# Expert weights in transfers of one whole matrix each: 2 MB as 128 runs of 16 KB in place of 512 runs of 4 KB, in a ring of eight slabs

## What is computed

```python
def hier_moe(x, w_rg, b_rg, w_re, b_re, w1, w3, w2):
    ...
    def expert_block(args):
        xb, e = args
        hdn = jax.nn.silu(xb @ w1[e]) * (xb @ w3[e])
        return hdn @ w2[e]
```

## Time and profile before

| | before |
|---|---|
| median of 3 runs | 1940.58 us (1939.97 to 1940.86) |
| the profiled execution | 1940.22 us, of which its span is 1938.4 us |
| PE busy | 1519.8 us, 78% of the span |
| DVE, ACT busy | 615.2 us, 420.9 us |
| DMA | 525.01 MB, 271 GB/s over the span |
| TensorE clock granted, mean | 0.916 of full |

### The profile page before, as it was taken

One profiled execution on the slowest core, in us unless ns is written; L12 is line 12 of the kernel. 1 busy time (PEld: TensorE's weight loads), 2 busy tenths in 40 slices (PEclk: granted clock), 3 DMA queues, 4 the chain that ended last, 5 costly groups with the idle time before them and its releaser, 6 DMA issues.

```text
span 1938.4 us, 22240 instructions
## 1 busy us (share of the span) xinstructions
PE 1519.8 (78%) x9046; PEld 1056.9 (55%) x9046; DVE 615.2 (32%) x1084; ACT 420.9 (22%) x616; POOL 4.7 (0%) x5
## 2 busy tenths in 40 slices
PE   7998979666666666666666567665999999989996
PEld 7788768522333123321333223331788878769996
DVE  3687931510111001110111101110453568244653
ACT  3554020410010000100100001000421332234542
POOL 0000000000000000000000000000000000000000
PEclk9999989788898889988998889888999999989998
DMA  9432344199999999999999999999432314325530
GB/s 318 156 131 96 143 151 183 41 365 410 409 410 410 410 410 410 410 410 409 410 410 410 410 410 410 410 409 400 174 126 87 131 44 174 123 96 189 195 116 23
DMA packets 164418, 525.01 MB, mean 271 GB/s; under 512 B 6514, under 2 KB 14834, under 8 KB 164356
## 3 DMA queue, kind: packets, MB, share of 16 engines
q1 hardware_dynamic: 164048, 523.39, 69.8%
q10 hardware_dynamic: 308, 0.78, 0.1%
HBM read 523.10 MB, written 1.05 MB: 270 GB/s over the span
## 4 chain that ended last, share of the span: by engine, by line
PE 55%; DMA 20%; DVE 10%; SPq 9%; ACT 2%; issue 2%; DVEq 0%; ACTq 0%
DMA ring<-in_w 20%; PE psum L323 15%; SPq L1259 9%; PE psum L998 6%; PE psum L1013 5%; PE psum L381 5%; PE psum L382 5%; PE psum L383 5%; PE psum L1042 3%; DVE arena L746 3%; PE psum L1032 3%; PE psum L344 2%; PE psum L603 1%; DVE shared L1757 1%; PE psum L1394 1%
## 5 line engine op out<-in xcount | busy, mean ns | idle before, releaser
L1013 PE MATMUL psum<-ring,arena 128*32 128x512 f32 x1536 | 224.9, 722 | 133.3 <-DMA ring<-in_w 119.2
L381 PE MATMUL psum<-parts 128*128 128x256 f32 (+1 forms) x832 | 246.2, 296 | 11.4 <-DVE parts L459 6.8
L382 PE MATMUL psum<-parts 128*128 128x256 f32 (+1 forms) x832 | 243.2, 292 | 0.0
L383 PE MATMUL psum<-parts 128*128 128x256 f32 (+1 forms) x832 | 243.1, 292 | 0.0
L323 PE MATMUL psum<-arena,ring 128*128 128x256 f32 x960 | 214.9, 386 | 11.8 <-DMA ring<-in_w_in 11.3
L323 PEld LDWEIGHTS psum<-arena,ring 128*128 128x128 f32 x960 | 184.9, 194 | 38.5 <-issue 13.0
L1013 PEld LDWEIGHTS psum<-ring,arena 128*32 128x32 f32 x1536 | 49.9, 125 | 285.3 <-DMA ring<-in_w 174.1
L381 PEld LDWEIGHTS psum<-parts 128*128 128x128 f32 x832 | 161.6, 194 | 20.6 <-issue 13.7
L383 PEld LDWEIGHTS psum<-parts 128*128 128x128 f32 x832 | 162.0, 195 | 2.1
L382 PEld LDWEIGHTS psum<-parts 128*128 128x128 f32 x832 | 162.0, 195 | 1.9
L1213 DVE TENSOR_TENSOR shared<-shared,psum 128x512 f32<-128x512 f32 x16 | 11.0, 687 | 460.7 <-PE psum L1013 460.7
(11 more groups left out here) (207 smaller groups left out, 1451.3 us busy)
## 6 DMA issues: line engine op xcount, KB each, us to landing
ring<-in_w SPq DMA_DIRECT2D x128, 2048.0 KB, 23.6
shared<-in_w SPq DMA_DIRECT2D x64, 2048.0 KB, 23.4
ring<-in_w_in SPq DMA_DIRECT2D x18, 2048.0 KB, 8.8
ring<-in_w_ffn_gate_up SPq DMA_DIRECT2D x11, 2048.0 KB, 8.0
ring<-in_w_gate SPq DMA_DIRECT2D x8, 2048.0 KB, 8.9
ring<-in_w_ffn_down SPq DMA_DIRECT2D x5, 2048.0 KB, 7.8
ring<-in_w_out SPq DMA_DIRECT2D x4, 2048.0 KB, 8.1
ring<-in_w_gla_out SPq DMA_DIRECT2D x2, 2048.0 KB, 8.2
```

The costliest lines, as they stand in the source:

```text
L381: pe.matmul(out, w[0], x[0], start=start, stop=False)
L382: pe.matmul(out, w[0], x[1], start=False, stop=False)
L383: return pe.matmul(out, w[1], x[0], start=False, stop=stop)
L1013: m = pe.matmul(ps[slots, bank, :], V.picked[:, k, slots], part[:, e, j, :], start=(k == 0), stop=(k == DT - 1))
```

## The change

It makes one transfer out of one whole matrix of one expert (16 KB in one run for each partition), and a ring of eight slabs, counted over a pair of quads (24 slabs). The ring has two places more, slots 6 to 7 and 8 to 9 of `shared`; what lay there (the router's numbers, the memory's squares and root) moves to other slots. PE waits for each of a product's four slabs at the first contraction tile, and frees each at the last one. Eight loads are issued ahead of the loop, not six. The loop over quads becomes one over pairs of quads, with the body in a function.

```diff
@@ block1_pe @@
-    for i in (2, 3):
-        pe.drain().then_inc(S(f"moe_read{i}"), 1)
+    for i in (0, 1):
+        pe.drain().then_inc(S(f"moe_read{i}"), FREED)
...
         pe_slab_tiles(K, pe, B, R, f"co{s}", tiles("co", 4 * s, 4), cu)
-        pe.drain().then_inc(S(f"moe_read{s}"), 1)
+        pe.drain().then_inc(S(f"moe_read{2 + s}"), FREED)
+        if s == 0:
+            pe.drain().then_inc(S("moe_read4"), FREED)
...
-        pe.drain().then_inc(S(f"moe_read{4 + s}"), 1)
+        pe.drain().then_inc(S(f"moe_read{5 + s}"), FREED)
+    pe.drain().then_inc(S("moe_read7"), FREED)
...
-CUTS = 4
-SETS = [(name, cut) for name in ("w1", "w3", "w2") for cut in range(CUTS)]
-RSETS = RING
+SLABS3 = [(name, e) for name in ("w1", "w3", "w2") for e in range(QUAD)]
+RSLABS = 8
+PAIR = 2
+USES = PAIR * len(SLABS3) // RSLABS
+FREED = 2
+PLACES = (4, 5, 2, 3, 6, 0, 1, 7)
...
+    def wait_landed(self, eng, n, i):
+        eng.wait_ge(self.landed(i), n * (16 * USES) + 16 * (i // RSLABS + 1))
+    def wait_passed(self, eng, n, i):
+        eng.wait_ge(self.passed(i), n * USES + i // RSLABS + FREED + 1)
@@ moe_pe @@
-            for w, bank in enumerate(MOE_BANK["up"]):
-                for cut in range(CUTS):
-                    i = CUTS * w + cut
-                    pe.wait_ge(S(f"moe_landed{i % RSETS}"), n * 32 + 16 * (i // RSETS + 1))
-                    part = moe_set(K, i, DT // CUTS)
-                    for j in range(DT // CUTS):
-                        k = DT // CUTS * cut + j
-                        for e in range(QUAD):
-                            slots = slice(e * SLOTS, (e + 1) * SLOTS)
-                            m = pe.matmul(ps[slots, bank, :], V.picked[:, k, slots], part[:, e, j, :],
-                                          start=(k == 0), stop=(k == DT - 1))
-                    m.then_inc(S(f"moe_read{i % RSETS}"), 1)
+        for name, bank in zip(("w1", "w3"), MOE_BANK["up"]):
+            at = [ring.index(half, name, e) for e in range(QUAD)]
+            w = [ring.slab(i, DT) for i in at]
+            for k in range(DT):
+                for e in range(QUAD):
+                    if k == 0:
+                        ring.wait_landed(pe, pair, at[e])
+                    slots = slice(e * SLOTS, (e + 1) * SLOTS)
+                    m = pe.matmul(ps[slots, bank, :], V.picked[:, k, slots], w[e][:, k, :],
+                                  start=(k == 0), stop=(k == DT - 1))
+                    if k == DT - 1:
+                        m.then_inc(ring.passed(at[e]), 1)
...
@@ moe_sp @@
-    w = {name: d[name].rearrange("e (p h k) n -> h p e (k n)", p=P, h=CUTS) for name in ("w1", "w3", "w2")}
+    w = {name: d[name].rearrange("e (p k) n -> p e (k n)", p=P) for name in ("w1", "w3", "w2")}
...
-        sp.dma_start(moe_set(K, i, 1).rearrange("p e k n -> p e (k n)"), w[name][cut, :, bass.ds(first, QUAD), :])\
-          .then_inc(S(f"moe_landed{i % RSETS}"), 16)
+        sp.dma_start(ring.slab(i, 1), w[name][:, bass.ds(first + (i // len(SLABS3) * QUAD + e), 1), :])\
+          .then_inc(ring.landed(i), 16)
-    for i in (2, 3, 0, 1, 4, 5):
-        load(i, 0, 1)
+    for i in range(RSLABS):
+        load(i, 0, 0, FREED)
...
-    sp.wait_ge(S("moe_read1"), rounds * NQ * 2 + 1)
+    sp.wait_ge(ring.passed(3), rounds * pairs * USES + FREED)
```

More of the change, by code:

```diff
@@ L972, in moe_pe @@
     pe.wait_ge(S("mem_squares"), 1)
[L973 removed]
+    pe_group(K, pe, B, "mem_ms", [K.c("j1024")] * DT, [K.tiles(3, DT)[:, j, :] for j in range(DT)])
     pe.wait_ge(S("chosen"), 1)
@@ L1045, in moe_pe @@
+    with pe.Fori(0, rounds) as r:
+        with pe.Fori(0, NQ // PAIR) as q:
+            for half in range(PAIR):
+                quad(r * (NQ // PAIR) + q, half)
     pe.drain().then_inc(S("moe_over"), 1)
@@ new lines, in moe_dve, with quad @@
+    ring = MoeRing(K)
+    last_of = lambda half, name: ring.index(half, name, QUAD - 1)
+    def quad(pair, q, half):
+        n = pair * PAIR + half
+        first = q * (PAIR * QUAD) + half * QUAD
+        for t in range(TT):
+            dve.tensor_tensor(by_slot(V.sel[:, t, :]), wide(K.c("slot_iota"), QUAD),
+                              last(V.place[:, t, bass.ds(first, QUAD)], SLOTS), ALU.is_equal).then_inc(S("sel_built"), 1)
+        dve.wait_ge(S("sel_built"), n * 4 + 2)
+        for t in range(TT):
+            dve.tensor_tensor(by_slot(V.wsel[:, t, :]), by_slot(V.sel[:, t, :]),
+                              last(V.weight[:, t, bass.ds(first, QUAD)], SLOTS), ALU.mult).then_inc(S("sel_built"), 1)
+        dve.wait_ge(S("picked"), n * 2 + 1)
+        dve.tensor_copy(K.A(3, 512), ps[:, MOE_BANK["pick"][0], :]).then_inc(S("picked_dve"), 1)
+        dve.wait_ge(S("silu"), n + 1)
+        ring.wait_passed(dve, pair, last_of(half, "w3"))
+        dve.tensor_tensor(V.hidden, V.hidden, ps[:, MOE_BANK["up"][1], :], ALU.mult).then_inc(S("gated"), 1)
+        ring.wait_passed(dve, pair, last_of(half, "w2"))
+        dve.tensor_copy(K.A(4, 512, 1024), ps[:, MOE_BANK["down"][0], :]).then_inc(S("y_dve"), 1)
+        for j, bank in enumerate(MOE_BANK["put"]):
+            dve.wait_ge(S("put"), n * 4 + j + 1)
+            part = K.A(2, 512, 512 * j)
+            dve.tensor_tensor(part, part, ps[:, bank, :], ALU.add).then_inc(S("total_added"), 1)
+        dve.wait_ge(S("total_added"), n * 4 + 5)
@@ L1223, in moe_dve @@
+    with dve.Fori(0, rounds) as r:
+        with dve.Fori(0, NQ // PAIR) as q:
+            for half in range(PAIR):
+                quad(r * (NQ // PAIR) + q, q, half)
         ins = dve.tensor_scalar(K.A(5, TT * NE, 576), K.A(5, TT * NE, 576), -float(SLOTS), None, ALU.add)
```

234 lines of the change are left out of this document (118 added, 116 removed).

## The result

| | before | after |
|---|---|---|
| median, 4 runs each on one chip | 1940.28 us (1938.07 to 1940.86) | 1896.50 us (1891.92 to 1900.74) |
| the profiled execution | 1940.22 us, span 1938.4 | 1897.18 us, span 1895.4 |
| PE busy | 1519.8 us | 1558.4 us |

The ratio of after to before is 0.978, with a 95% interval of 0.9765 to 0.9795: faster, by 43.8 us where 32 were forecast. The time lies inside the range, in the middle of its lower half.

A forecast was written before the change was run, and what follows sets the result against it. DMA was taken to bound the expert stage. 396.6 + 0.3 + 3.7 + 184 x 4.94 (909.0) + 8.7 = 1318.3 against 1350.7, 32.4 us earlier, so 1940.2 became about 1908 us; range 1886 to 1930.

The forecast's parts named there:

- The bound and the mechanism: Expert stage: DMA sets the pace at 410 GB/s; 16 KB packets pay the 9.5 ns price per packet less often.
- The slab: Expert stage: one 2.097 MB transfer was to take 4.94 us (424.5 GB/s) for 5.12 before, with 184 left to move.
- consts2's 415 GB/s: Only row with packets above 4 KB: 81 packets of 7680 B over 1.5 us, meaning 5.05 us a slab.
- the two long rows: DMA rates in long runs, 387 GB/s for 2 KB packets and 410 for 4 KB; continued to 16 KB, 4.89 us a slab.
- The second argument: Mid-transfer rates of 400 and 425 GB/s give 4.70 us of data, plus 0.19 us per transfer: 4.89 us a slab.
- The start: Expert stage's beginning: first load in the loop 5.3 us later, at 396.6 plus 0.3, but eight slabs early, not six.
- the drains: First block on PE: two more drains, 0 to 0.7 us in all, taken as 0.3.
- Worth 2 x 5.12 = 10.2 us: Two more slabs loaded early, in DMA's idle stretch between 340 and 390 us, leave 184 to move, not 186.
- The end: After the last landing all of w2's product remains: 8.7 us, bounds 7.1 to 13.6, where one cut took 3.39.
- All behind it is unchanged: Everything after the last w2 product, the second block included, was to keep its time, so the 32.4 us carry through.
- The PE loop: Rival, chance 0.05: low clock stretches w2's landing to w1's release, loop 65.5 us, 2007 us total; expected loop 54.1 under 59.3.
- the latency: Term of the loop between PE and DMA in each quad: 2.7 us, 7.8 to landing for a lone slab less 5.1 of data.

The follow-up runs named there:

- e3: The changed kernel with two experts' matrices in one 4 MB transfer, still in 16 KB runs: median 1893.31 us, ratio 0.9769.
- e2: The changed kernel with the seventh and eighth loads held back until w1's first slab is freed: median 1907.97 us, ratio 0.9837.
- e9: The changed kernel with five unread matmuls before the second block's 2.35 us wait and 32 products widened from 8 to 64 columns: 1892.55 us.
- e4: The changed kernel with the last quad's w2 loaded in four cuts of 4 KB per expert: median 1894.06 us, ratio 0.9768.
- the two edits: In the second block, five unread matmuls before the 2.35 us wait, and 32 products widened from 8 to 64 columns; on the kernel of before, 1932.96 us.
- e11: The kernel of before with five unread matmuls before the second block's 2.35 us wait and 32 products widened to 64 columns: 1932.96 us, ratio 0.9968.

## Why the prediction was right, and where its sizes were off

**The bound and the mechanism were right.** The stage was bound by DMA, a run of 16 KB goes as one packet, and the price of a packet is paid once for it. The run with 4 KB packets shows that nothing else in the change makes up the gain.

**The slab was mis-sized**, and this is most of the error. The sum took 4.94 us, "a third of the way to the one short row that speaks against them", consts2's 415 GB/s over 1.5 us. Measured are (1302.3 - 397.0 - 3.7) / 184 = 4.90 us, or 428 GB/s. The line through the two long rows had said 4.89, and 429. So 7.4 us of the 10.6 us by which the forecast was above the profiled pair come from having let 81 packets outvote two long rows. The second argument, from 3 us at 425 GB/s, gave the same 4.89 by way of a cost per transfer that e3 shows not to be there; that it agreed was chance, and should not have counted as support.

**The start was right, in part by luck.** Forecast 396.9 for the first load in the loop, measured 397.0. But w1's product starts at 389.62 for 389.00, 0.6 us later where 0.3 was taken for the drains, and the load goes out 0.33 us after its end where 0.53 was taken; the two misses cancel. (PE's times ahead of the stage differ by 0.6 us the other way at 278 us, before any of the drains added, so the 0.6 need not be their price.) "Worth 2 x 5.12 = 10.2 us" is, at the new rate, 9.8, and e2 shows 9.2 to 11.5.

**The end was a little low.** 8.7 us forecast for the last product, 9.5 measured: in it the low clock lasts for about 5 us, not for the 3.4 of one cut. This differs between executions; in e9 the same product takes 8.5. e4 shows that it is on the path, and that taking it away gives only 2.4 us as long as the clock is left to fall.

**Together** the stage ends at 1311.9 for 1318.3: +0.1, -7.4 and +0.8.

**The second block was not in the forecast at all.** "All behind it is unchanged" holds of the code, not of the time: 4.3 us of the profiled pair are the granted clock around the wait of 2.35 us, and 3.4 us of the medians go away with the two edits, which is not clear of the noise. The sum was made from one execution of before that had met both low stretches, and did not allow for that.

**The PE loop did not decide**, as forecast, but the margin was smaller than I had worked out, 1.5 to 4.8 us over the quads, 3.2 in the mean, for 5.2. The steps that failed are the low clock "for some 4 us" in w2's product, which held for 5 at 714.9 and cost 1.0 us more, 0.6 in the mean; w1's product "takes 7.1", taken from a quad in which the clock was full, where it takes 8.8 in six quads of fifteen; the latency, 3.3 for 2.7; and the slab, since the faster DMA is, the less time PE has. With 0.05 on this rival I was lucky rather than right: some 4 us more of PE work in a quad take back about half of the gain.

The Trainium skill (DMA: Bandwidth & Descriptors, Bandwidth) has 425 GB/s for a load of 16 MB, issued from GpSimd, under a fabric ceiling of 435. The runs here, whose loads SP issues, stay under the ceiling with 428 over 750 us, and are above the 425. The Trainium skill (the same page, SWDGE vs HWDGE vs iDMA) has a packet at 4096 B or less "preferably", where it describes what GpSimd builds. For these loads of SP the runs go against such a preference: 4 KB gives 410 GB/s here and 16 KB 428, and where page and measurement differ the measurement decides.

## What to carry to other kernels

Where a stream of loads sits on a plateau, fit a price per packet and a price per byte to the longest rows of two packet lengths, and carry the line on; don't bend it for a row of 1.5 us. When loads come in larger pieces, work out separately what more of them can be early (here 9 to 11 us), what is left to do after the last one lands (here 9.5 us), and the loop from landing to release in the longest of several quads, since the products at the low clock make it differ from quad to quad (here 31.0 to 34.3 us). And before a few us are put down to a change, look for a wait or a row of narrow products on PE behind which the granted clock differs between executions.

## What had not been expected of the hardware

- Doubling a transfer from 2 to 4 MB and halving the completion packets changes the rate by nothing that can be seen (321.28 and 321.33 MB in 750 us).
- Added PE work can pay for part of itself: with the selection done twice, the product behind it takes 8.7 us in one quad of fifteen, and without in six; in the others it takes 7.05.
- The step between the columns that the selection reads shows in its time: 5.3 us for 32 entries with a step of 2 elements of 4 B, 7.5 with 4 and 7.6 with 8.
- The clock can be low while PE is busy without a gap: 0.72 over 12 us, around 32 products of 8 columns, in some executions and 1.00 in others. Executions of the unchanged kernel on these chips spread from 1932.8 to 1942.1 us. With both edits e9 still spreads over 2.8 us and e11 over 6.2, so they hold only part of it; what the rest is stays open. The mean granted clock does not tell it: six of 39 executions of the unchanged kernel had 0.85 to 0.87 and took 1936.5 to 1941.0 us, no longer than the others with 0.90 to 0.92.
